# Second pass of the axial sample scores as two 64-row products on the two halves of the matrix rows

## What is computed

```python
def attend(qi):
    s = jnp.einsum('bqkgd,bskd->bkgqs', qi, k).astype(jnp.float32) * scale
    p = jax.nn.softmax(s, axis=-1).astype(v.dtype)
    return jnp.einsum('bkgqs,bskd->bqkgd', p, v)
```

## Time and profile before

| | us |
|---|---|
| median of 3 runs | 3666.42 |
| lowest and highest | 3663.82, 3667.58 |
| profiled execution, its own time | 3664.1 |
| profiled execution, span from first to last instruction | 3662.2 |
| mean granted TensorE clock | 0.954 of full speed |

### The profile page before, as it was taken

The page is one execution under the profiler, slowest core; times in us unless marked ns, Lnnn a source line. Parts: engine busy times, 40 slices in busy tenths (PEclk is TensorE's granted clock), DMA queues, the critical chain, the costliest instruction groups (busy, mean ns, idle before and its releaser), DMA issues. The chain is left out here.

```text
span 3662.2 us, 52032 instructions
## 1 busy us (share of the span) xinstructions
PE 3321.3 (91%) x19000; PEld 2782.5 (76%) x19000; DVE 2546.5 (70%) x4038; ACT 2031.1 (55%) x2823; POOL 390.2 (11%) x313
## 2 busy tenths in 40 slices
PE   8995779599999999988987899989879999999993
PEld 7873468499999999976863456558769999999992
DVE  4988945776676766747766788875666676666765
ACT  3117842266666666643437788762246666666664
POOL 0000011101111111102210000000111111011102
PEclk9998889799999999998998999999889999999996
DMA  3001223577777877753322110013287777777764
GB/s 126 30 32 42 67 77 117 172 252 251 250 241 243 255 248 250 233 170 111 108 77 76 35 41 23 23 42 121 103 265 245 235 255 249 256 242 237 255 219 158
DMA packets 361096, 588.85 MB, mean 161 GB/s; under 512 B 17680, under 2 KB 284048, under 8 KB 359440
## 3 DMA queue, kind: packets, MB, share of 16 engines
q1 hardware_dynamic: 339728, 511.75, 41.7%
q0 software_dynamic: 14336, 50.34, 6.3%
q10 hardware_dynamic: 6912, 25.17, 1.7%
HBM read 505.42 MB, written 78.64 MB: 159 GB/s over the span
## 5 line engine op out<-in xcount | busy, mean ns | idle before, releaser
L1251 PE MATMUL h_ps<-xT,high 128*128 128x384 f32 x3584 | 1067.1, 360 | 2.8 <-DVE xT L1373 2.8
L1369 DVE TENSOR_TENSOR low<-raw,high 128x2048 fp32r<-128x2048 f32 x384 | 877.0, 2285 | 155.0 <-ACT high L1313 148.1
L1252 PE MATMUL h_ps<-xT,low 128*128 128x192 f32 x3584 | 905.8, 253 | 0.0
L1313 ACT ACTIVATE high<-raw 128x2048 fp32r<-128x2048 f32 x384 | 734.7, 1914 | 283.7 <-PE yp_ps L1284 175.8
L1252 PEld LDWEIGHTS h_ps<-xT,low 128*128 128x128 f32 x3584 | 685.2, 191 | 1.3
L1251 PEld LDWEIGHTS h_ps<-xT,high 128*128 128x128 f32 x3584 | 676.2, 189 | 5.1 <-issue 3.6
L1429 DVE TENSOR_TENSOR gate_up<-h_ps,cross 128x384 f32<-128x384 f32 x256 | 142.8, 558 | 310.0 <-ACT cross L1332 306.3
L1332 ACT ACTIVATE cross<-h_ps 128x384 f32<-128x384 f32 x256 | 125.5, 490 | 278.0 <-PE h_ps L1255 277.9
L200 DVE SCALAR_TENSOR_TENSOR cat<-glu,taps,cat 128x272 f32<-128x272 f32 (+33 forms) x480 | 256.8, 607 | 0.0
L1928 DVE TENSOR_REDUCE col<-s_ps 128x1 f32<-128x1024 f32 (+1 forms) x192 | 200.5, 1044 | 62.8 <-PE s_ps L1874 62.3
L1971 ACT ACTIVATE p<-s_ps,col 128x1024 f32<-128x1024 f32 (+1 forms) x192 | 186.4, 971 | 57.9 <-DVE col L1928 57.8
(11 more groups left out here) (250 smaller groups left out, 6005.8 us busy)
## 6 DMA issues: line engine op xcount, KB each, us to landing
raw<-moe_w_gate SPq DMA_DIRECT2D x128, 1024.0 KB, 5.6
raw<-moe_w_up SPq DMA_DIRECT2D x128, 1024.0 KB, 8.0
raw<-moe_w_down SPq DMA_DIRECT2D x128, 1024.0 KB, 8.6
rows_x<-x ACTq DMA_DIRECT2D x24, 512.0 KB, 2.6
rows_acc<-ax ACTq DMA_DIRECT2D x24, 512.0 KB, 2.7
r<-rows_acc SPq DMA_DIRECT2D x24, 512.0 KB, 4.1
rows_qT_parts<-q_turned SPq DMA_DIRECT2D x12, 1024.0 KB, 4.0
q<-rows_qT_parts SPq DMA_DIRECT2D x24, 512.0 KB, 3.8
```

The costliest lines, as they stand in the source:

```text
L1251: nc.tensor.matmul(ps, wh[:, n, k, :], xT[:, u, k, :, :].rearrange("p s n -> p (s n)"), start=(k == 0), stop=False)
L1252: nc.tensor.matmul(ps[:, 0:SLOTS], wl[:, n, k, :], xT[:, u, k, 0, :], start=False, stop=False)
L1313: nc.scalar.activation(split_view(high, at), piece_view(at), ACT.Copy).then_inc(high_ready, 1)
L1369: nc.vector.tensor_tensor(split_view(low, at), piece_view(at), split_view(high, at).bitcast(F32), ALU.subtract).then_inc(low_ready, 1)
```

## The change

`qk` does the first pass (q against k high, 128 rows) for all blocks first. Its second pass then takes only q high times k low: for block 0 the rows 0 to 63 of `q` against rows 0 to 63 of the low slot, for block 1 rows 64 to 127 of a new tile `q_again` (which holds q high once more) against rows 64 to 127 of the low slot. The two products stand on different halves of the array's rows and write different PSUM banks. The product q low times k low is dropped. In the prompt, with its one block, the second pass is a single product on rows 0 to 63.

`q_again` has one tile for each side. One lies at `under_picks`, an address that is free in this stage, the other is a new allocation. `load` issues a second DMA (64 rows) per side, 24 in all, and PE waits for both.

```diff
+        q_again = [nc.alloc_sbuf_tensor_at("q_again0", [P, SET * P], F32R, offset=under_picks), c.sb("q_again1", [P, SET * P], F32R)]
...
                         sp.dma_start(q[:, side, :].bitcast(F32), m["qT_parts"][bass.ds(t * P, P), side * SET * P:(side + 1) * SET * P]).then_inc(q_in[side], 16)
+                        sp.dma_start(q_again[side][DH:P, :].bitcast(F32), m["qT_parts"][bass.ds(t * P, DH), side * SET * P:(side + 1) * SET * P]).then_inc(q_in[side], 16)
...
-                            pe.wait_ge(q_in[side], tile * 16 + 16)
+                            pe.wait_ge(q_in[side], tile * 32 + 32)
                         pe.wait_ge(expd, number(tile, side, n + 1))
-                        for b in range(nk // HALF):
-                            at = first * P + b * HALF
-                            for part in range(2):
-                                last = nc.tensor.matmul(s_ps[n % 2][:, b * HALF:(b + 1) * HALF], q[:, side, n * P:(n + 1) * P],
-                                                        keys[:, part * AX_KV + 2 * side + n // SHARE, at:at + HALF], start=(part == 0), stop=(part == 1))
+                        blocks = range(nk // HALF)
+                        kv, of = 2 * side + n // SHARE, slice(n * P, (n + 1) * P)
+                        cols = [slice(b * HALF, (b + 1) * HALF) for b in blocks]
+                        at = [slice(first * P + b * HALF, first * P + (b + 1) * HALF) for b in blocks]
+                        for b in blocks:
+                            nc.tensor.matmul(s_ps[n % 2][:, cols[b]], q[:, side, of], keys[:, kv, at[b]], start=True, stop=False)
+
+                        turned = q[:, side, :], q_again[side]
+                        for b in blocks:
+                            rows = slice(DH * b, DH * (b + 1))
+                            last = nc.tensor.matmul(s_ps[n % 2][:, cols[b]], turned[b][rows, of], keys[rows, AX_KV + kv, at[b]], start=False, stop=True)
```

More of the change, by code:

```diff
@@ L1776, in _, with axial_attention @@
                         low(t - 1)
-def axial_attention(c, m, keys, values, cat, early):
+def axial_attention(c, m, keys, values, cat, early, under_picks):
     nc = c.nc
@@ L2105, in trunk @@
             early = [early_weight(under_keys, k) for k in range(3)]
-            axial_attention(c, m, keys, values, cat, early)
+            axial_attention(c, m, keys, values, cat, early, under_picks)
             project_out(c, m, 1, early, m["x2"], cat, picks, keys[:].rearrange("p k n -> p (k n)"))
```

## The result

The changed kernel takes 3695.03 us (median of 6 runs, 3691.58 to 3696.3) against 3664.44 us (median of 6 runs, 3662.45 to 3667.58) of the kernel before: a ratio of 1.0079, 95% interval 1.0069 to 1.0089, so 30.6 us slower. The forecast was +24.1 us, 3690.5, with a range of 3662 to 3720.

What follows compares the result with a forecast made beforehand. PE was taken to bound the units with a `pv` step; sample 14.0, prompt 9.6 and first units 0.5 sum to +24.1 us, 3688.2 from the profiled execution, 3690.5 with the median 2.3 above it; range 3662 to 3720.

Steps and rivals of the forecast that it cites:

- The bound: Score stage: PE bounds the units with a `pv` step, 3.00 us each in the sample and 2.10 in the prompt.
- The change of shape: Score products: a change of shape waits until the array is empty; 0.43 us into the 64-row pair, 0.38 out to transposes.
- Rival A: Second pass: no drain between full and half rows; sample unit 2.775 us, sample −26.6 us, total 3640; chance 0.14.
- B: Changes of shape cost only 0.095 us each; sample −4.1, prompt +5.3, total 3668; chance 0.09 together with unsplit rows.
- The overlap: Sample's second pass: two 64-row products on opposite halves cost one product plus 0.01 us, saving 0.225 a unit.
- Rival C: Sample's second pass: drains but no overlap of the fp32r, 512-column products; 27.3 us more, total 3718; chance 0.05.
- Sample +14.0: Sample: 118 units with `pv` steps and scores, each 0.119 us longer, period 3.12, +14.0 us.
- prompt +9.6: Prompt: one 64-row product alone saves nothing; +0.344 us in each of 28 `pv` units, +9.6 us.
- Cover in the units without `pv`, 0: Prompt units without `pv`: the added time lies in the 0.57 us in which PE waits anyway; 0 added.
- the prediction's own sign of being wrong: Wrong if the prompt's units without `pv` grew from 1.62, or the pair's record followed 0.23 after the full product.
- Rival D: Prompt: PE's clock falls to 1.2 GHz as PE idles; 28 `pv` units near 4.5 us, +58, 3748; chance 0.02.
- The start, +0.5: First units of each group have their scores in front of everything, +0.5 us; the extra loads' wait taken as 0.

Runs made afterwards that it cites:

- three pairs: Kernel before, with all the sample's score products in three pairs of 64 rows (q high·k high, q high·k low, q low·k high), prompt as before: 3655.0 us, ratio 0.9972.

## Why the prediction was right

The forecast was +24.1 us, and +30.6 was measured, inside a range of 58 us. The terms for the sample and the prompt's settled sets held to within 1 us, and they carry seven tenths of the time. The rest, some 9 us of clock and start, wasn't foreseen; that it left the result inside the range owes something to the range's width. The time itself, 3695.0 against 3690.5, looks closer than the difference: the forecast added 2.3 us to the profiled execution from a median of three, and over six the median stands 0.3 above it.

**The bound.** PE at 3.00 in the sample and 2.10 in the prompt's `pv` units: right. Each nanosecond added on PE came out in the period (0.12 in the sample, and 0.35 in a settled `pv` unit of the prompt).

**The change of shape.** The step that decided the sign: that going to half the rows and back costs time, read off L511 and L1889. The figures for in (0.43) and out (0.38) were measured as such, and the kernels that differ by one change each gave 0.20 and 0.15. Rival A (no drain between row shapes) fell with them; B (0.095 each) too. What the runs show is the price. That it is the array emptying stays an inference from the records.

**The overlap.** Taken from float32 pairs of 384 columns, it holds for fp32r pairs of 512: 0.23 a unit. Rival C fell.

**Sample +14.0, prompt +9.6.** Measured 14.3 and 8.7. The prompt's term was a little too large because the first `pv` unit of a set is cushioned: 0.19 there instead of 0.34. The time by which the loads are asked for ahead was misread (a prompt set takes 15 to 16 us, not 17), without effect, as none of the later loads was waited for.

**Cover in the units without `pv`, 0.** Right at full clock. At 1.2 GHz it failed, and with it came the prediction's own sign of being wrong: the records grow, PE's 0.57 of idle time is gone, and the unit is 2.20 long, in the first set and in two units of the second.

**The clock.** This is the term that was mis-sized, 0 instead of 8.1 us. Rival D, with 0.02, had the place, and its price for a `pv` unit at 1.2 GHz (near 4.5, measured 4.4 and 4.1), but as all or nothing (+58) and by another mechanism: a clock that falls because PE idles. What came was a clock that rises late with PE busy, in the first set and half of the second. The prediction read the clock from a slice of 91.6 us with 0.8 in it, which hides that the stage starts at 1.2 GHz and stays there until 1943 even in the kernel before; it should have asked what the stage's first 20 us, with PE cold and little work in it, would do when the array is half empty.

**The start, +0.5 instead of 1.7.** The first wait took the second DMA in full and more. The relief I set against it (the keys' copies being later) didn't show: with the loads the first product came 6.2 to 7.7 after the first issue in eight kernels (7.1 in the mean), without them 5.3 to 5.8 in five (5.6).

**Between the groups, 0 instead of −0.9.** Luck of the two executions that were profiled: the clock was low there for longer in the one of the kernel before.

## What to carry to other kernels

Count the changes of the array's shape (rows by columns of the stationary operand) in an inner loop as instructions of their own, and read their price from places in the trace where such a change stands already. Splitting a product into two halves side by side saves one product's time; it pays when the neighbours have that shape too, as in three pairs in a row, and not when a single pair stands between full products. Steps that look like a burden on one engine can be the cover under which another works: two `pv` steps together saved changes of shape and lost 39 us. Where PE starts cold and its work is thin, keep half-array products out of the first microseconds.

## What the runs showed of the hardware

A change of shape costs 0.15 us (half rows or half columns to 128-column transposes, transposes to half columns) to 0.20 us (into a score product with 128 weight columns) at 2.4 GHz, alike for rows and for columns. 64-row products on opposite halves of the rows, fp32r and 512 columns long, overlap wholly: a pair takes 0.23 us. TensorE's granted clock can stay at 1.2 GHz for tens of microseconds while the profile shows PE nearly always busy, when 64-row products are part of that work: from the first product at 1935.5 to 1966 in the changed kernel, from 2072 to 2106 where all of the sample's scores were on 64 rows. With full rows in the prompt it rose 6 to 9 us after the first product. It isn't the 64-row products alone: in the three pairs the sample's first set lost under 1 us to it. The Trainium skill's page "TensorEngine Tiling (Array Packing)" (Key Properties) says that changing the tiling mode, not just the tile, drains TensorE. The 0.15 to 0.20 us at every change here agree with it, though no run shows what the array does in that time.
